# A hybrid decoder step on one core: one region of on-chip memory for all stages, loads moved across the stage ends, and another order of the prompt's query tiles

## The reference, cut to what matters

```python
def prompt_layer(x, p_emb, W, tb):
    nq, nkv, ng, fq, fk, fv, logf, ga, gb = project(x, W['w_in'], W['b_forget'])
    kc, vc, cpos, ks, vs, ov = nsa_prepare(nkv[:, :, :4], W)
    c = jnp.cumsum(logf, axis=1)
    def block(args):                       # one tile of 128 queries
        ...
        o_n = nsa_block(q_b, qpos, g_b, kc, vc, cpos, ks, vs, ov, kw_b[:, :, 0], kw_b[:, :, 1], wpos, tb)
        o_f = fox_block(fq_b, qpos, c_b, fk, fv, c, kpos)
        return o_n, o_f
    o_n, o_f = lax.map(block, ...)         # 8 tiles
    mix = merge(from_blocks(o_n), from_blocks(o_f), ga, gb, W)
    y, conv_state = finish_layer(x, mix, p_emb, ...)
```

## Time and profile before

| | us |
|---|---|
| median of 3 runs | 2786.87 |
| profiled execution, its own time | 2786.2 |
| its span, first to last instruction | 2784.3 |
| PE busy | 2633.3 (95% of the span) |
| DVE, ACT, POOL busy | 710.7, 547.6, 359.4 |
| stage 1, until | 240 |
| stage 2, until | 402 |
| stage 3, until | 845 |
| stage 4, until | 1168 |
| stage 5, until | 2784.3 |

### The profile page before, as it was taken

The page is one execution under the profiler, slowest core; times in us unless marked ns, Lnnn a source line. Parts: engine busy times, 40 slices in busy tenths (PEclk is TensorE's granted clock), DMA queues, the critical chain, the costliest instruction groups (busy, mean ns, idle before and its releaser), DMA issues.

```text
span 2784.3 us, 29412 instructions
## 1 busy us (share of the span) xinstructions
PE 2633.3 (95%) x10923; PEld 1475.7 (53%) x10923; DVE 710.7 (26%) x1927; ACT 547.6 (20%) x1328; POOL 359.4 (13%) x573
## 2 busy tenths in 40 slices
PE   8998988889886888899999999999999999999999
PEld 4554654555555566566665445555555554444443
DVE  0000016656662244211011222222222220101222
ACT  0001015556552233100000221011111110010110
POOL 0000005345343000100000330000000000021110
PEclk9999988999997999899999999999999999999999
DMA  4114631021008866601030311111111115223300
GB/s 165 56 49 121 201 97 66 1 80 33 1 1 174 249 207 188 206 23 45 23 105 20 74 38 31 45 30 34 42 30 45 30 60 180 99 98 113 142 30 30
DMA packets 198343, 227.15 MB, mean 82 GB/s; under 512 B 52063, under 2 KB 149823, under 8 KB 196807
## 3 DMA queue, kind: packets, MB, share of 16 engines
q1 hardware_dynamic: 191418, 199.80, 23.9%
q0 software_dynamic: 5648, 16.33, 1.7%
q10 hardware_dynamic: 1168, 9.58, 1.0%
HBM read 203.60 MB, written 37.99 MB: 87 GB/s over the span
## 4 chain that ended last, share of the span: by engine, by line
PE 58%; ACT 0%; DVE 0%; issue 0%; DVEq 0%
PE ps L1962 23%; PE ps L2012 11%; PE ps L1912 9%; PE ps L2058 5%; PE ps L1915 4%; PE ps L1935 4%; PE ps L2016 1%; PE ps L1900 1%; PE ps L2061 0%; PE ps L1939 0%; PE ps L1969 0%; ACT arena L2148 0%; PE ps L1947 0%; PE ps L2042 0%; DVE arena L2270 0%; DVE qfT L2287 0%
## 5 line engine op out<-in xcount | busy, mean ns | idle before, releaser
L1962 PE MATMUL ps<-xT,qT 128*128 128x480 f32 (+1 forms) x2112 | 648.1, 469 | 0.0
L1962 PEld LDWEIGHTS ps<-xT,qT 128*128 128x128 f32 x2112 | 344.5, 191 | 296.4 <-issue 296.4
L2012 PE MATMUL ps<-arena 128*128 128x512 f32 x704 | 305.3, 593 | 0.0
L1912 PE MATMUL ps<-xT,arena 128*128 128x363 f32 (+1 forms) x768 | 244.8, 472 | 2.6 <-DVEq L2198 2.6
L2012 PEld LDWEIGHTS ps<-arena 128*128 128x128 f32 x704 | 132.6, 190 | 167.2 <-issue 166.7
L159 PE MATMUL ps<-w_rows,xT 128*128 128x512 f32 (+1 forms) x512 | 200.8, 550 | 5.0 <-DMA w_rows<-in_w_in 3.5
L1912 PEld LDWEIGHTS ps<-xT,arena 128*128 128x128 f32 x768 | 146.7, 191 | 92.7 <-DVEq L2198 2.8
L763 PE MATMUL ps<-ident,probs 128*128 128x128 f32 x816 | 139.4, 304 | 25.0 <-POOL probs L925 12.5
L874 ACT ACTIVATE probs<-probs,nmax 128x640 f32<-128x640 f32 (+7 forms) x192 | 143.0, 745 | 98.3 <-DVE nmax L836 49.5
L159 PEld LDWEIGHTS ps<-w_rows,xT 128*128 128x128 f32 x512 | 96.6, 191 | 98.8 <-issue 92.0
L2232 DVE TENSOR_SCALAR qfT<-qfT 128x480 f32<-128x480 f32 (+1 forms) x88 | 35.1, 420 | 443.7 <-ACT qfT L2107 443.7
(11 more groups left out here) (304 smaller groups left out, 2626.3 us busy)
## 6 DMA issues: line engine op xcount, KB each, us to landing
arena<-in_w_ffn_down SPq DMA_DIRECT2D x66, 512.0 KB, 3.5
arena<-in_cache_fox_kv SPq DMA_DIRECT2D x64, 256.0 KB, 6.1
xT<-in_cache_fox_kv SPq DMA_DIRECT2D x64, 256.0 KB, 6.8
arena<-in_cache_nsa_kv SPq DMA_DIRECT2D x64, 192.0 KB, 4.7
qT<-in_w_ffn_up SPq DMA_DIRECT2D x22, 512.0 KB, 4.0
qT<-in_w_ffn_gate SPq DMA_DIRECT2D x22, 512.0 KB, 5.3
bias_rows<-rev_dram ACTq DMA_DIRECT2D x8, 1160.0 KB, 19.7
arena<-in_w_in SPq DMA_DIRECT2D x16, 512.0 KB, 5.3
```

What stands on the lines that cost most here:

```text
L1912: pe.matmul(ps[:, 4 * (j % 2) + side, 0:n], at.w_gate[e][:, side, c, :], x[:, c, t0:t0 + n], start=(c == 0), stop=(c == KD - 1))
L1962: mm = pe.matmul(ps[:, 2 * (j % 3) + side, 0:n], at.w_ug[e][:, side, c, :], x[:, c, t0:t0 + n], start=(c == 0), stop=(c == KD - 1))
L2012: mm = pe.matmul(ps[:, q + h, :], hT[:, c, t0:t0 + m], at.w_down[:, load % RING, cols], start=(c == 0), stop=(c == NFF - 1))
```

## The change: what it does

`arena` is allocated first and holds the tiles of all stages; `EarlyLayout` gives the offsets for stages 1 to 3. With that:

- SP loads the first NSA and FoX query weights in stage 1, right behind `w_rows`, and no longer at the start of stage 2.
- SP loads `bias_slc` of turn 0 at the end of stage 2, ahead of the store of `neg_sums`, and no longer at the start of stage 3.
- At the end of SP's list in stage 3 it loads the compressor's weights (once DVE is done with the last tile's second CMP pair) and key pages 0 to 3 of round 0 (once it is done with the last tile's second WIN pair). Both leave stage 4.
- The last row tile (the requests' new rows) is written by stage 1 straight into `newT` and `v_new`; the five POOL copies at L427 to L431 go.
- Query tiles are taken in the order 6, 0, 5, 1, 4, 2, 3, 7 in both turns, and the buffers rotate by that order.
- The copies into `rawT` (2 of ACT and 2 of DVE in stage 2, 8 of ACT and 8 of DVE in each of the 4 rounds of stage 4) run through the same elements in another order: the write is contiguous and the read from PSUM has a step of 8 elements. Before, the read was contiguous and the write had a step of 64 elements.

All tiles of the arena have the name `arena` in the changed kernel's rows.

```diff
+class EarlyLayout:
+
+
+    def __init__(self, arena):
+        self.w_rows = view(arena, 0, KD, W_N)
+        self.fk = view(arena, 24064, FW)
...
+        self.w1, self.w2, self.pe = view(arena, 4640, 2, 16, P), view(arena, 8736, 2, HD), view(arena, 8864, 2, 16)
...
+        self.bias_slc = view(arena, 0, 2, 2, T)
+        self.bias_fox, self.diag_fox, self.causal = view(arena, 4224, 2, 2, T), view(arena, 8320, 2, 4, P), view(arena, 9344, P)
...
+def query_weights(eng, at, io, g, kind, there):
+
+    w_in = io["w_in"][0].rearrange("(k p) f -> p k f", p=P)
+    if kind == FOX:
+        eng.dma_start(at.w_fox, w_in[:, :, C_FQ + g * P:C_FQ + (g + 1) * P]).then_inc(there, 16)
+        return
+    for kvh in range(NKVH):
+        c = C_NQ + kvh * NG * HD + g * HD
+        eng.dma_start(at.w_nsa[:, :, kvh * HD:(kvh + 1) * HD], w_in[:, :, c:c + HD]).then_inc(there, 16)
+
+
+def slc_bias(eng, at, io, turn, there):
+
+    for j in range(2):
+        for half in range(2):
+            eng.dma_start(at.bias_slc[:, half, j, :], bias_tile(io, half * NG + 2 * turn + j, False, P - T, P, T)).then_inc(there[j], 16)
...
+            query_weights(sp, at, io, 0, SLC, keep.wn_in)
+            query_weights(sp, at, io, 0, FOX, keep.wf_in)
...
+            slc_bias(sp, at, io, 0, keep.slc_in)
...
-            nc.gpsimd.tensor_copy(keep.newT[:, 0:4, :], keep.fkT[:, :, T:R]).then_inc(kept_new, 1)
-            nc.gpsimd.tensor_copy(keep.newT[:, 4:6, :], keep.keyT[:, :, T:R]).then_inc(kept_new, 1)
-            nc.gpsimd.tensor_copy(keep.v_new[0:64, 0:FW], keep.fv[0:64, NTP, :]).then_inc(kept_new, 1)
-            nc.gpsimd.tensor_copy(keep.v_new[0:64, FW:FW + P], keep.v_slc[0:64, NTP, :]).then_inc(kept_new, 1)
-            nc.gpsimd.tensor_copy(keep.v_new[0:64, FW + P:FW + 2 * P], keep.v_win[0:64, NTP, :]).then_inc(kept_new, 1)
...
-        done = turn * NTP + i
+        done = self.done = turn * NTP + TILE_ORDER.index(i)
...
+TILE_ORDER = (6, 0, 5, 1, 4, 2, 3, 7)
+FIRST_TILE, LAST_TILE = TILE_ORDER[0], TILE_ORDER[-1]
 ORDER = ((CMP, 0), (SLC, 0), (SLC, 1), (WIN, 0), (CMP, 1), (WIN, 1), (FOX, 0), (FOX, 1))
 GROUPS, BIG = (SLC, CMP, WIN, FOX), (SLC, WIN, FOX)
-PAIRS = [Pair((t * NTP + i) * 8 + x, t, i, br, j)
-         for t in range(2) for i in range(NTP) for x, (br, j) in enumerate(ORDER)]
+PAIRS = [Pair((t * NTP + y) * 8 + x, t, i, br, j)
+         for t in range(2) for y, i in enumerate(TILE_ORDER) for x, (br, j) in enumerate(ORDER)]
...
-    return (turn * NTP + i) * 8 + ORDER.index((branch, j))
+    return (turn * NTP + TILE_ORDER.index(i)) * 8 + ORDER.index((branch, j))
...
-            sp.wait_ge(io["toeplitz_done"], 16 * 8)
             for turn in range(2):
                 if turn:
-                    sp.wait_ge(logits_done, 2 * pair_no(0, NTP - 1, CMP, 1) + 2)
-                for j in range(2):
-                    for half in range(2):
-                        sp.dma_start(bias_slc[:, half, j, :],
-                                     bias_tile(io, half * NG + 2 * turn + j, False, P - T, P, T)).then_inc(slc_in[j], 16)
+                    sp.wait_ge(logits_done, 2 * pair_no(0, LAST_TILE, CMP, 1) + 2)
+                    slc_bias(sp, at, io, turn, slc_in)
                 if turn:
-                    sp.wait_ge(logits_done, 2 * pair_no(0, NTP - 1, WIN, 1) + 2)
+                    sp.wait_ge(logits_done, 2 * pair_no(0, LAST_TILE, WIN, 1) + 2)
                 for half in range(2):
                     for j in range(2):
                         sp.dma_start(bias_win[:, half, j, :],
...
+            sp.wait_ge(logits_done, 2 * pair_no(1, LAST_TILE, CMP, 1) + 2)
+            compressor_weights(sp, ahead, io, keep.cw_in)
+            sp.wait_ge(logits_done, 2 * pair_no(1, LAST_TILE, WIN, 1) + 2)
+            for p in range(4):
+                key_pages(sp, ahead, io, keep.first_ids, 0, p, keep.k_in)
...
-            def set_diagonal(turn, i):
-                if i == 0:
-                    pool.wait_ge(fox_in, 64 * turn + 64)
-                if i >= 2:
-                    pool.wait_ge(logits_done, 2 * pair_no(turn, i - 2, FOX, 1) + 2)
-                nc.gpsimd.tensor_tensor(diag_fox[:, i % 2], bias_fox[:, :, :, i * P:(i + 1) * P].rearrange("p h j n -> p (h j) n"),
+            def set_diagonal(p):
+                if p.i == FIRST_TILE:
+                    pool.wait_ge(fox_in, 64 * p.turn + 64)
+                if p.done % NTP >= 2:
+                    pool.wait_ge(logits_done, 2 * pair_no(p.turn, TILE_ORDER[p.done % NTP - 2], FOX, 1) + 2)
+                nc.gpsimd.tensor_tensor(diag_fox[:, p.done % 2], bias_fox[:, :, :, p.i * P:(p.i + 1) * P].rearrange("p h j n -> p (h j) n"),
...
+def compressor_weights(sp, at, io, there):
+
+    for kv in range(2):
+        sp.dma_start(at.w1[:, kv], io["nsa_cmp_w1"][0, kv].rearrange("(l two) d k -> (two d) l k", two=2)).then_inc(there, 16)
+        sp.dma_start(at.w2[:, kv], io["nsa_cmp_w2"][0, kv]).then_inc(there, 16)
+
+
+def fox_page(io, page, kv):
+    return io["cache_fox_kv"][0, bass.ds(page, 1)].rearrange("o t k h d -> (o t) k (h d)")[:, kv, :]
+
+
+def key_pages(sp, at, io, ids, n, p, there):
+
+    for r in range(2):
+        sp.dma_start(at.pages[:, p % 4, r, :], fox_page(io, ids[n, r, p], 0)).then_inc(there[p % 4], 16)
+
+
...
-            for p in range(4):
-                keys(0, p)
...
-                    for kv in range(2):
-                        sp.dma_start(at.w1[:, kv], io["nsa_cmp_w1"][0, kv].rearrange("(l two) d k -> (two d) l k", two=2)).then_inc(cw_in, 16)
-                        sp.dma_start(at.w2[:, kv], io["nsa_cmp_w2"][0, kv]).then_inc(cw_in, 16)
...
-                    ins = nc.scalar.copy((at.rawT_v if kv else at.rawT_k)[par * HD:(par + 1) * HD, h].rearrange("p f m -> p m f"),
-                                         ps[h * HD:(h + 1) * HD, ring.bank(n, name), :].rearrange("p (m f) -> p m f", f=8))
+                    ins = nc.scalar.copy((at.rawT_v if kv else at.rawT_k)[par * HD:(par + 1) * HD, h],
+                                         ps[h * HD:(h + 1) * HD, ring.bank(n, name), :].rearrange("p (m f) -> p f m", f=8))
...
-                    ins = nc.vector.tensor_copy((at.rawT_v if kv else at.rawT_k)[par * HD:(par + 1) * HD, 2 + h].rearrange("p f m -> p m f"),
-                                                ps[h * HD:(h + 1) * HD, ring.bank(n, name), :].rearrange("p (m f) -> p m f", f=8))
+                    ins = nc.vector.tensor_copy((at.rawT_v if kv else at.rawT_k)[par * HD:(par + 1) * HD, 2 + h],
+                                                ps[h * HD:(h + 1) * HD, ring.bank(n, name), :].rearrange("p (m f) -> p f m", f=8))
...
-        with ExitStack() as early:
-            keep.fkT = sb(early, "fkT", [P, 4, RP])
-            keep.keyT = sb(early, "keyT", [P, 2, RP])
-            keep.v_slc = sb(early, "v_slc", [P, NT, P])
-            keep.v_win = sb(early, "v_win", [P, NT, P])
-            keep.fv = sb(early, "fv", [P, NT, FW])
-            keep.ff = sb(early, "ff", [P, NT, 8])
-            project_rows(k, keep, io)
-            keep.kcT = sb(early, "kcT", [P, 64])
-            keep.vc = sb(early, "vc", [64, P])
-            prepare_prompt(k, keep, io)
-            prompt_attention(k, keep, io)
-        arena = sb(ctx, "arena", [P, ARENA])
+        arena = keep.arena = sb(ctx, "arena", [P, ARENA])
+        at = keep.early = EarlyLayout(arena)
+        keep.fkT, keep.keyT, keep.v_slc, keep.v_win, keep.fv, keep.ff = at.fkT, at.keyT, at.v_slc, at.v_win, at.fv, at.ff
+        keep.kcT, keep.vc = at.kcT, at.vc
+        project_rows(k, keep, io)
+        prepare_prompt(k, keep, io)
+        prompt_attention(k, keep, io)
```

152 lines of the change are left out of this document (70 added, 82 removed).

## The result

The changed kernel takes 2737.13 us (median of 4 runs, 2732.05 to 2740.72), the kernel before 2785.47 in the runs beside it (2783.59 to 2788.81). The ratio is 0.9824, 95% interval 0.9803 to 0.9844: 48 us or 1.8% faster. I had forecast 22 us, and the time lies outside my range.

What follows compares the result with a forecast made beforehand. PE, 95% busy, was taken as the bound, with gains possible only in its first 1168 us. Terms 5.3 + 6.0 - 8 + 18.5 + 0 = 22 us off 2786.2 gave 2764 us; range 2740 to 2785, 8 times in 10.

Steps and rivals of the forecast that it cites:

- The copies, 0 forecast: Copies into `rawT`: price taken as unchanged, 0 us; bounds 13.9 us gained and 5 us lost.
- So a stepped read costs extra as well: Copies into `rawT`: step from a stepped SBUF read, 1.4 ns an element against 1.2 contiguous, to 0 us gained.
- the copies get cheap: Rival on the copies into `rawT`: waits of 13 us go, giving 2751 us; chance 0.18.
- Stage 3, 2 us lost forecast (6.0 - 8): Stage 3: 6.0 us gained at its start by the early bias, 8 us lost by the new tile order.
- The work is the same, so only the steps between tiles count: Tile order, stage 3: six steps up and six down over two turns, 8 us lost; bounds 18 lost, 10 gained.
- My cost of a step up: Stage 3, small tile followed by a wide one: three pairs each late by 1.0 us, 3.0 us a step.
- Stage 4's loads, 18.5 us forecast: Head of stage 4: 13.3 us gained up to the values, then a 5.23 us key page wait gone; bounds 9 and 24.
- raw rows at 883: Stage 4, round 0: PE's raw rows arrive at 883 in place of 891.19, 8 us sooner with eight key loads moved.
- my 6.0: Start of stage 3: waits of 12.8 us replaced by 6.8, 6.0 us gained; bounds 1 and 10.
- Seam 1, 5.3 us: Seam of stages 1 and 2: 4.7 us of idle time and 0.6 of slow product gained; bounds 4 and 7.
- its second term: First NSA product of stage 2: 28 matmuls each 20 ns faster after the shorter idle time, 0.6 us.
- the next wait would stay at 3.59 us: Stage 2: PE's wait for `w_nsa` of g = 2, 3.59 us at 330.61, expected to stay.

Runs made afterwards that it cites:

- e2: The changed kernel with the old copies into `rawT` (read in order, stepped write) put back; 2752.53 us, ratio 0.9893 to the kernel before.
- e4: The kernel before with one edit alone, the new copies into `rawT` (contiguous write, stepped read); 2771.68 us, ratio 0.9960.
- e8: The changed kernel with `bias_slc` of turn 0 loaded at the start of stage 3 again; 2746.14 us, ratio 0.9863 to the kernel before.
- e1: The changed kernel with its query tiles back in the order 0 to 7; 2739.67 us, ratio 0.9853 to the kernel before.
- e14: The changed kernel with query tiles in the order 0 to 7, run once more; 2743.15 us, ratio 0.9840 to the kernel before.
- e3: The changed kernel with the compressor's weights and key pages 0 to 3 of round 0 loaded in stage 4 again; 2766.89 us, ratio 0.9930.
- e10: The changed kernel with the compressor's weights alone loaded in stage 4 again; 2753.69 us, ratio 0.9893 to the kernel before.
- e12: The changed kernel with the first group's query weights loaded in stage 2 again; 2744.50 us, ratio 0.9856 to the kernel before.
- e15: The changed kernel with the store of x_turned in stage 2 cut into parts, half issued at the old place; 2737.14 us, ratio 0.9823.

## Why the prediction was wrong

The sum failed in three places: the price of the copies, TensorE's clock in stage 3, for which it had no term, and the size of what the loads give.

- **The copies, 0 forecast: wrong.** They are worth 12.5 us in stage 4 by e2 and 10.2 by e4, near my upper bound of 13.9. The failed step is "So a stepped read costs extra as well". The nearest row was a stepped read of SBUF by another operation of DVE, and it says nothing of PSUM. What costs is the stepped write to SBUF: 1030 ns became 580 and 688. The Trainium skill ("Advanced Engine Details and Errata", Memory Cachelines) wants every two consecutive PSUM elements contiguous for best throughput. For these copies that did not show: ACT's with the stepped read takes 580 ns, as a contiguous one of the same shape does. The rival "the copies get cheap", at 0.18, had the cause right, with 13 us.
- **Stage 3, 2 us lost forecast (6.0 - 8): wrong, 13.8 us gained.** The waits came out nearly as priced. At the start they fell from 12.8 to 6.1 us, 6.7 where I said 6.0. The steps between tiles cost 44.5 - 38.2 = 6.3 us where I said 8. The two cancel, and idle time stayed at 54 us. The failed step is "The work is the same, so only the steps between tiles count". The same 2752 matmuls took 374.35 us in place of 387.84, since the granted clock rose from .90 to .95. The sum had no term for that, though the trace of the kernel before has it: 0.51 and 0.55 in the first two stretches of 20 us of stage 3, where the kernel after has 0.91 in both. e8 shows the part that hangs on the bias: 9.0 us in medians, more than the waits alone. How much of the rest is chance is open. Ten profiles in the new order with the early bias have a mean busy time of 377.5 us, the two of the stage as it was before 387.84 and 381.22, which makes some 7 us.
- **The order by itself.** It loses 5 us at the steps and gives 3 back at the start, as e1 and e14 show, and in time no loss is left (2.7 us the other way, with a standard error of 2.4). So undoing it did not win back the 8 us that the sum took off for it. My cost of a step up was near: 0.98 and 1.58 us of waits ahead of tile 5's first wide scores, where I said 3.0.
- **Stage 4's loads, 18.5 us forecast: right in mechanism, mis-sized.** e3 shows 23.7 us, at my upper bound of 24. The mis-sized term is the head of the stage. I had the first compressor run 8.2 us sooner (raw rows at 883), and against e3 it is 13.1: the raw rows are 9.7 us sooner, and PE's wait of 4.1 us for the compressor's weights themselves is gone too. My sum had none for them. The kernel before shows no such wait, since PE comes there later, but e10 has 6.1 and e4 6.0 us. From the first compressor run to the second I had counted 5.2 us for the values and 5.2 for key page 4, 10.4, and e3 shows 11.0.
- **Start of stage 3 in the order 0 to 7.** e1 and e4 differ by 6.4 us, but that this is my 6.0 is luck: only 1.1 us of it are idle time.
- **Seam 1, 5.3 us: right** (5.1 by e12), but not its second term. My 0.6 us for a slow product was a misreading: the row of 28 matmuls in the earlier trace rows was the head of a run of 48, cut off by the view's window. The whole product took 16.35 us before and takes 16.57 now:

```profile
246.09 16.35 PE L441 MATMUL ps<-xT,w_nsa 128*128 128x363 f32 x48 [8.01 <-DMA w_nsa<-in_w_in]
```

That the next wait would stay at 3.59 us was wrong in the profile, 6.55. But it is 5.83 in e4 too, and 3.59 was one execution's number.

With the measured terms, 5.1 + 6.7 - 6.3 + 7 + 23.7 + 12.5 = 49 us, beside 48 measured. It agrees better than it should. Undone one by one the medians give more, and each term is uncertain by some 3 us. The 54 us of the profiles hold a further part of chance: stage 3 of kernels with the same instructions took 425.7 to 437.2 us.

The wrong terms all pointed the same way, and I had added them as if sure. Cheap copies (13 us) and an order that costs nothing (8 us) would have put the forecast at 2743, and each was among the rivals only by itself.

## What to carry to other kernels

Price a stepped access by the memory and the side it is on: where a copy runs from PSUM to SBUF, put the step on the PSUM read and keep the SBUF write contiguous. A load moved out of a full DMA queue is worth what it delays in every list entry behind it, until the queue has caught up, so follow the queue a round further than the first wait. Don't read an edit of a few us from one profile here; compare idle time, which is steady, apart from busy time, which follows the clock. Where an edit removes a long wait, look at the clock behind the wait too, and give it a term.

## What the runs showed of the hardware

- A copy of 64x512 from PSUM with an eight-element step in the read takes 580 ns on ACT and 688 on DVE, a contiguous one 580 and 682; with a 64-element step in the SBUF write it takes 1030 on both.
- In the new order with the early bias PE's idle time in stage 3 was 53.6 to 54.7 us in ten profiles. Its busy time there for the same instructions ran from 371.58 us (e15, at a mean granted clock of .96) to 383.50 (e3, .92).
- A store of 4608 KB held SP's queue for 22.19 us while ACT's 9.3 MB of copies were under way. Half of its bytes held it for 21.98 us, and with the store asked for by another engine a 6 KB store held it for 27.87 us.
